# The adaLN projection moved from TensorE to GpSimd, and another order of rows in attention's output projection

## The chip, the cores and the metric

The kernel runs on one core of one Trainium2 chip. The metric is the device time of one execution in microseconds (us). A core has five engines that run side by side and wait for each other through semaphores: TensorE (PE; its weight loads are PEld), VectorE (DVE), ScalarE (ACT), GpSimd (POOL) and SyncE (SP), whose queue issues the weight loads from HBM here.

## The reference

Batch 1, 256 tokens, width 1024. A first block of two layers (pooling with attention and a gated FFN with a short convolution; RG-LRU and the same FFN) is followed by a second block whose two norms and two residuals are modulated (adaLN). The part of the reference that this change touches is `mod`; all it reads are the conditioning vector and its own weights, so it may be computed at any time before the second block:

```
x = first_block(x, ...)
c_act = silu(c)                                   # 1024 numbers
mod = c_act @ ada_w[l] + ada_b[l]                 # 1024 x 6144, in fp32
sh1, sc1, gt1, sh2, sc2, gt2 = split(mod, 6)
h = rms_norm_2(x, norm_mix_g[l]) * (1 + sc1) + sh1
...                                               # four mixers, merged
x = x + gt1 * (merged @ w_o[l])
h = rms_norm_2(x, norm_ffn_g[l]) * (1 + sc2) + sh2
x = x + gt2 * (square(relu(h @ ffn_w1[l])) @ ffn_w2[l])
```

Attention's output is `concat(pool_out, attn_out) @ pa_w_out`: 1024 rows, in 8 tiles of 128, by 1024 columns. Each FFN of the first block takes 1024 to 2 x 2816 columns (22 pairs of column tiles m and m + 22), convolves, gates, and goes back through 22 x 8 tiles.

## The kernel before

**Products.** All activations stand with features on the 128 partitions and the 256 tokens in the free dimension. Each large product is made of three fp32r matmuls (high x high, high x low, low x high). So every weight chunk of 128 x 1024 goes through three steps: SP loads it into a slot of `ring` (NR = 9 slots, in the order that `weight_order()` writes out), ACT rounds it to `whi` (NS = 7 buffers, 1 instruction), DVE subtracts to get `wlo` in place of the ring's slot (1 instruction with two operands in SBUF), and PE uses the two in 24 matmuls of 256 columns. One FFN column m of the input side is two chunks, m and m + 22: 48 matmuls.

**Order.** Each engine's program is written out by hand in the same nesting of stages: `pool_attn`, `conv_ffn(0)`, `rglru`, `conv_ffn(1)`, `mixers`, `relu_ffn`. ACT and DVE convert ahead through `feed(c)`, which goes up to AHEAD = 5 (DVE) or 6 (ACT) entries of the weight order past entry c; entries of the adaLN matrix count there, though nothing is converted for them. SP issues entry n when entry n - 9 has been used (`used`), strictly in order, so one late user holds all later loads. DVE's instructions of one FFN column are: subtract (`wlo`) for a later chunk, two taps of the convolution on `zu` (one operand in PSUM, one in SBUF), `wlo`, two taps on `zg`, then `hidl` and the product `zg<-zg,zu` (each with two operands in SBUF).

**adaLN.** The matrix `ada_w` is 48 chunks of 128 x 1024. A call of `mod_step` on PE takes two of them: four fp32 matmuls, each of 32 equal columns `sc32` (silu(c), spread) against 512 columns of the chunk, straight from the ring, accumulated in PSUM over 8 calls. Eight calls make a third of `mod`; ACT copies it to `mrow` and `mod_turn` turns it with four transposes. The 24 calls stand as `("A",)` in the table ATTN (7) and after the first column tile of attention's output projection (1), in `rglru` by ADA_RG (8), and in `conv_ffn(1)` by ADA_IN (8).

**End of attention.** The projection `pa_w_out` reads the tiles `pah`/`pal` 0 to 7. Tiles 4 to 7 come from the head pairs (steps O), 0 to 3 from the pooling groups (steps G, in the order 3, 2, 1, 0), and `linear` reads them in the order 0 to 7 for the first two column tiles together.

**GpSimd** adds the squares for the norms (`add_squares`, 6 small adds a norm), makes the masks and the pooling sums early in attention, and multiplies ten tiles in `rglru`.

## Time and profile before

| | |
|---|---|
| median of 3 runs | 1161.66 us (1161.20 to 1168.12) |
| the profiled execution, its own time | 1161.85 us |
| its span in the profile | 1160.0 us |
| PE busy, weight loads | 1091.7 us (94%), 1036.3 us (89%) |
| DVE, ACT, POOL busy | 835.9 us (72%), 641.7 us (55%), 66.7 us (6%) |
| mean granted TensorE clock | 0.976 |
| HBM read | 197.99 MB, 172 GB/s over the span |

The span is 1.85 us shorter than the execution's own time, and that in turn is 0.19 us over the median. A share of busy time is a mean over stages; the stages here run one after another: attention to 101 us, its output projection to about 134, the first FFN to 331, RG-LRU to 455, the second FFN to 655, then the second block.

### The profile page before, as it was taken

What the parts mean: (1) busy time and instruction counts of PE and PEld (TensorE: products, weight loads), DVE (VectorE), ACT (ScalarE), POOL (GpSimd) and SP (SyncE); (2) the same over time, 40 slices, a digit from 0 to 9 for tenths busy, and PEclk for the clock granted to TensorE, in tenths of its full rate; (3) what the DMA queues carried; (4) which work ended last, traced back from release to release, by engine and by line L of the source; (5) the groups of instructions that cost most, each with busy time, mean ns of one, the idle gap of its engine ahead of it and who ended that gap; (6) DMA issues with size and microseconds to landing.
All of it is one profiled execution on the core that took longest, in us unless ns stands there. A gap on an engine that the chain in (4) does not pass through costs nothing.

```text
span 1160.0 us, 21002 instructions
## 1 busy us (share of the span) xinstructions
PE 1091.7 (94%) x8588; PEld 1036.3 (89%) x8588; DVE 835.9 (72%) x1444; ACT 641.7 (55%) x1098; POOL 66.7 (6%) x79
## 2 busy tenths in 40 slices
PE   6996999999999979999999989899999979999996
PEld 6874999999987779999999978799989979999996
...
GB/s 344 120 203 235 128 213 185 184 171 180 193 215 186 276 133 135 247 237 228 237 220 185 195 111 107 83 92 91 128 109 155 70 207 179 182 183 183 184 160 37
DMA packets 59857, 200.41 MB, mean 173 GB/s; under 512 B 6769, under 2 KB 11505, under 8 KB 59633
## 3 DMA queue, kind: packets, MB, share of 16 engines
...
HBM read 197.99 MB, written 1.05 MB: 172 GB/s over the span
## 4 chain that ended last, share of the span: by engine, by line
PE 81%; DVE 10%; ACT 6%; DMA 1%; issue 1%; ACTq 0%; SPq 0%; POOL 0%; DVEq 0%
PE ps L470 80%; DVE wlo L1552 2%; ACT whi L1037 1%; ACT L1037 1%; DVE xr L1558 1%; DMA ring<-pa_w_out 1%; DMA ring<-pa_w_in 1%; ACT xr L1037 1%; DVE cosT L1552 1%; ACT rr L1037 0%; DVE rst L1581 0%; DVE raw L1552 0%; DVE bks L1552 0%; DVE hl L1552 0%; ACT sc L1037 0%
## 5 line engine op out<-in xcount | busy, mean ns | idle before, releaser
L470 PE MATMUL ps<-hh,whi 128*128 128x256 f32 (+1 forms) x1656 | 481.1, 291 | 18.1 <-DVE wlo L1552 15.6
L470 PE MATMUL ps<-hh,wlo 128*128 128x256 f32 (+1 forms) x1656 | 471.3, 285 | 0.0
L470 PE MATMUL ps<-hl,whi 128*128 128x256 f32 (+1 forms) x1656 | 469.4, 283 | 0.0
L1552 DVE TENSOR_TENSOR wlo<-ring,whi 128x1024 fp32r<-128x1024 f32 (+1 forms) x313 | 376.1, 1216 | 73.8 <-ACT whi L1037 73.2
L1037 ACT ACTIVATE whi<-ring 128x1024 fp32r<-128x1024 f32 (+1 forms) x313 | 321.6, 1039 | 68.7 <-PE ps L470 52.6
L470 PEld LDWEIGHTS ps<-hh,whi 128*128 128x128 f32 x1656 | 316.6, 191 | 39.0 <-issue 31.2
L470 PEld LDWEIGHTS ps<-hl,whi 128*128 128x128 f32 x1656 | 317.1, 192 | 1.3 <-issue 1.0
L470 PEld LDWEIGHTS ps<-hh,wlo 128*128 128x128 f32 x1656 | 316.7, 191 | 0.0
L470 PE MATMUL ps<-hidh,whi 128*128 128x256 f32 x608 | 172.2, 283 | 0.0
L470 PE MATMUL ps<-hidh,wlo 128*128 128x256 f32 x608 | 172.1, 283 | 0.0
L470 PE MATMUL ps<-hidl,whi 128*128 128x256 f32 x608 | 172.1, 283 | 0.0
L470 PEld LDWEIGHTS ps<-hidh,whi 128*128 128x128 f32 x608 | 116.7, 192 | 0.8 <-issue 0.8
L470 PEld LDWEIGHTS ps<-hidl,whi 128*128 128x128 f32 x608 | 116.7, 192 | 0.0
L470 PEld LDWEIGHTS ps<-hidh,wlo 128*128 128x128 f32 x608 | 116.7, 192 | 0.0
L2329 POOL TENSOR_TENSOR sqa<-sqa,sqt 128x256 f32<-128x256 f32 x36 | 34.5, 960 | 950.3 <-ACT sqt L1037 950.3
L1037 ACT ACTIVATE sqt<-x 128x256 f32<-128x256 f32 x49 | 20.1, 414 | 74.0 <-DVE x L1552 36.3
L1558 DVE SCALAR_TENSOR_TENSOR zg<-ps,vec,zg 128x255 f32<-128x255 f32 x84 | 40.4, 481 | 23.7 <-ACT zg L1037 21.1
L1037 ACT ACTIVATE zg<-ps,vec 128x256 f32<-128x256 f32 x42 | 23.6, 562 | 44.7 <-PE ps L470 44.6
L1037 ACT ACT_TABLE_LOAD x35 | 44.9, 1283 | 6.1 <-issue 3.9
L1558 DVE SCALAR_TENSOR_TENSOR zu<-ps,vec,zu 128x255 f32<-128x255 f32 x80 | 38.5, 481 | 12.1 <-ACT zu L1037 9.5
L1037 ACT ACTIVATE zu<-ps,vec 128x256 f32<-128x256 f32 x40 | 22.5, 564 | 29.7 <-PE ps L470 21.0
L470 PE MATMUL ps<-yin,ring 128*128 128x256 f32 x160 | 38.6, 378 | 0.0
...
## 6 DMA issues: line engine op xcount, KB each, us to landing
...
```

The lines of the kernel that those rows point to most:

```text
L470: return e.matmul(o, l, r, start=start, stop=stop)
L1037: return e.activation(o, i, func, bias=bias, scale=scale, accum_out=acc)
L1552: return e.tensor_tensor(o, a, b, op)
L1558: return e.scalar_tensor_tensor(out=o, in0=a, scalar=s, in1=b, op0=op0, op1=op1)
L2329: e.tensor_tensor(sqa[:, :], sqa[:, :], sqt[:, m % 2, :], ADD).then_inc(*sum_g.up((n, m)))
```

## The change

The 48 chunks of `ada_w` are used by GpSimd. For each, `mod_piece` multiplies the 128 x 1024 chunk by its column of silu(c) (one scalar for each partition) in place in the ring, and adds it to the running sum `acc` (the first of eight writes `acc` directly and has no addition). PE only adds over the partitions: `mod_sum`, two fp32 matmuls of 32 columns of ones against 512 columns of `acc`, six times in all, and the same three `mod_turn`. All pieces stand in the two FFNs: one chunk after each of 20 columns of the input side, and one after each of the first four columns of the output side. Attention, its projection and RG-LRU have none. SP's ring waits for GpSimd where an `ada_w` entry is replaced. `pa_w_out` reads its tiles in the order 4, 5, 6, 3, 2, 7, 1, 0.

```diff
-ADA_IN = ((), (2, 5, 8, 11, 14, 17, 19, 21))
-ADA_RG = ((5, 7, 9), (1, 3, 5, 7, 8))
+ADA_IN = (range(2, 22), range(1, 21))
+ADA_OUT = range(4)
+ADA_SUM = ({12: 0, 20: 1}, {11: 3, 19: 4})
+ADA_LAST = ({6: 2}, {5: 5})
+ADA_TURN = ({21: 0}, {12: 1})
...
-    13, ("B", 1), ("S", 3), ("P", 2), ("T", 1), ("A",), 14, ("S", 4), ("P", 3), ("T", 2), 15, ("S", 5), ("P", 4), ("T", 3), ("A",),
-    3, ("V",), ("S", 6), ("P", 5), ("T", 4), 2, ("O", 0), ("S", 7), ("P", 6), ("T", 5), ("A",), 1, ("O", 1), ("P", 7), ("T", 6),
-    ("A",), 0, ("T", 7), ("O", 2), ("G", 3), ("A",), ("G", 2), ("A",), ("O", 3), ("G", 1), ("A",), ("G", 0),
+    13, ("B", 1), ("S", 3), ("P", 2), ("T", 1), 14, ("S", 4), ("P", 3), ("T", 2), 15, ("S", 5), ("P", 4), ("T", 3),
+    3, ("V",), ("S", 6), ("P", 5), ("T", 4), 2, ("O", 0), ("S", 7), ("P", 6), ("T", 5), 1, ("O", 1), ("P", 7), ("T", 6),
+    0, ("T", 7), ("O", 2), ("G", 3), ("G", 2), ("O", 3), ("G", 1), ("G", 0),
...
-    ada = iter(range(24))
-
-    def columns():
-        n = next(ada)
-        o.extend(("ada_w", n, z, 0) for z in range(2))
+    ada = iter(("ada_w", 8 * r + k, z, 0) for r in range(3) for z in range(2) for k in range(8))
...
             whole("pa_w_in", 8, (at,))
-        elif at[0] == "A":
-            columns()
-        if m == 1:
-            columns()
...
             if m in ADA_IN[l]:
-                columns()
+                o.append(next(ada))
         for m in range(8):
             whole(f"ffn_w_out{l}", 22, (m,))
+            if m in ADA_OUT:
+                o.append(next(ada))
...
+        acc = [alloc(st, "acc", [128, 2, 1024])] * 2
...
-            def linear(w, ms, of, nk, need):
+            def linear(w, ms, of, nk, need, rows=range(8)):
-                    for q in range(n):
+                    for i, q in enumerate(rows[0:n]):
...
-                            t = mm(o, wlo[c % NR][:, q, :], rh, False, k + q == nk - 1)
-                            if q == n - 1:
+                            t = mm(o, wlo[c % NR][:, q, :], rh, False, k + i == nk - 1)
+                            if i == n - 1:
                                 t.then_inc(*through.up(c))
...
-            def mod_step():
-                n = ada["n"]
-                ada["n"] += 1
-                r, k = n // 8, n % 8
-                if k == 0:
-                    take(("ada", r))
-                p = ps[where["ada", r]]
-                for z in range(2):
-                    c = number["ada_w", n, z]
-                    landed[c % NR].wait_ge(e, c)
-                    ada_dve.wait_ge(e, "sc32")
-                    for y in range(2):
-                        g = 2 * z + y
-                        t = mm(p[32 * g:32 * g + 32, :], sc32[:, k, :], ring[c % NR][:, 4 * y:4 * y + 4, :], k == 0, k == 7)
-                    t.then_inc(*through.up(c))
-                if k == 7:
-                    give(("ada", r), ada_act, r)
-                    ada["late"] = r
-
-            def mod_turn():
-                r, ada["late"] = ada["late"], None
-                if r is not None:
-                    p = take(("mod", r))
-                    ada_act.wait_ge(e, r)
-                    for q in range(4):
-                        t = e.transpose(p[:, q * 128:q * 128 + 128], mrow[:, q * 128:q * 128 + 128], ident)
-                    t.then_inc(*ada_pe.up(r))
-                    give(("mod", r), ada_dve, ("mod", r))
+            def mod_sum(h):
+
+                r, z = h // 2, h % 2
+                p = take(("ada", h))
+                ada_pool.wait_ge(e, number["ada_w", 8 * r + 7, z])
+                for y in range(2):
+                    g = 2 * z + y
+                    t = mm(p[32 * g:32 * g + 32, :], ones[:, 0:32], acc[h // 3][:, z, y * 512:y * 512 + 512])
+                t.then_inc(*ada_pe.up(("sum", h)))
+                give(("ada", h), ada_act, h)
+
+            def mod_turn(r):
+                p = take(("mod", r))
+                ada_act.wait_ge(e, 2 * r + 1)
+                for q in range(4):
+                    t = e.transpose(p[:, q * 128:q * 128 + 128], mrow[:, q * 128:q * 128 + 128], ident)
+                t.then_inc(*ada_pe.up(("turn", r)))
+                give(("mod", r), ada_dve, ("mod", r))
...
-                residual(1, "pa_w_out", 8, pair(pah, pal), lambda k: at_dve.wait_ge(e, ("pal", k)), also)
+                residual(1, "pa_w_out", 8, pair(pah, pal), lambda k: at_dve.wait_ge(e, ("pal", k)), None, (4, 5, 6, 3, 2, 7, 1, 0))
...
-                    if m in ADA_IN[l]:
-                        mod_step()
+                    if m in ADA_SUM[l]:
+                        mod_sum(ADA_SUM[l][m])
+                    if m in ADA_TURN[l]:
+                        mod_turn(ADA_TURN[l][m])
...
                 def also(m):
-                    mod_turn()
+                    if m in ADA_LAST[l]:
+                        mod_sum(ADA_LAST[l][m])
+                    if l == 1 and m == 6:
+                        mod_turn(2)
...
-                    if m in ADA_RG[0]:
-                        mod_step()
...
-                    mod_turn()
-                    if m in ADA_RG[1]:
-                        mod_step()
...
 
             if order[c][0] == "rg_w_out" and order[c][2] == 9:
                 rg_pe.wait_ge(e, ("out", 7))
+            elif order[c][0] == "ada_w":
+                ada_pool.wait_ge(e, c)
             else:
                 through.wait_ge(e, c)
...
+            def mod_copy(h):
+                r, z = h // 2, h % 2
+                rows = slice(64 * z, 64 * z + 64)
+                ada_pe.wait_ge(e, ("sum", h))
+                if r:
+                    ada_pe.wait_ge(e, ("turn", r - 1))
+                act(mrow[rows, :], ps[where["ada", h]][rows, :], ACT.Copy).then_inc(*ada_act.up(h))
...
+            def scale_of(n):
+                ada_dve.wait_ge(e)
+                stt(gsc[:, n, :], mod[:, 24 * n + 8:24 * n + 16], 1.0, P(("norm_mix2", "norm_ffn2")[n], 0, 8), ADD, MUL).then_inc(*ada_dve.up(("gsc", n)))
...
+                        scale_of(0)
+                    if l == 1 and m == 6:
+                        mod_turn(2)
+                        scale_of(1)
...
+            def add_square(n, m):
+                square.wait_ge(e, (n, m))
+                sum_g.wait_ge(e)
+                e.tensor_tensor(sqa[:, :], sqa[:, :], sqt[:, m % 2, :], ADD).then_inc(*sum_g.up((n, m)))
...
-                    e.tensor_tensor(sqa[:, :], sqa[:, :], sqt[:, m % 2, :], ADD).then_inc(*sum_g.up((n, m)))
+                    add_square(n, m)
+
+            pieces = iter((h, k) for h in range(6) for k in range(8))
+
+            def mod_piece():
+
+                h, k = next(pieces)
+                c = number["ada_w", 8 * (h // 2) + k, h % 2]
+                a, w = acc[h // 3][:, h % 2, :], ring[c % NR][:, :, :].rearrange("p a b -> p (a b)")
+                ada_dve.wait_ge(e, "silu")
+                landed[c % NR].wait_ge(e, c)
+                if k == 0:
+                    if h > 1:
+                        ada_pe.wait_ge(e, ("sum", h - 2))
+                    e.tensor_scalar(a, w, cpar[15][:, k:k + 1], None, MUL).then_inc(*ada_pool.up(c))
+                else:
+                    e.tensor_scalar(w, w, cpar[15][:, k:k + 1], None, MUL).then_inc(*ada_pool.up(("product", c)))
+                    ada_pool.wait_ge(e)
+                    e.tensor_tensor(a, w, a, ADD).then_inc(*ada_pool.up(c))
+
+            def squares_and_pieces(n):
+                for m in range(8):
+                    if m in ADA_OUT:
+                        mod_piece()
+                    if 0 < m < 7:
+                        add_square(n, m)
...
-            add_squares(2)
+            for m in ADA_IN[0]:
+                mod_piece()
+            squares_and_pieces(2)
             for m in range(10):
...
             add_squares(3)
-            add_squares(4)
+            for m in ADA_IN[1]:
+                mod_piece()
+            squares_and_pieces(4)
             add_squares(5)
```

The weight order of SP at the end of attention, before: entries of `ada_w` stand among the last chunks of `pa_w_in` and those of `pa_w_out` (the number behind `ring` tells the slot).

```order
L2378 DMA ring_19<-pa_w_in 128x1024
L2378 DMA ring_20<-ada_w 128x1024
L2378 DMA ring_21<-ada_w 128x1024
L2378 DMA ring_22<-ada_w 128x1024
L2378 DMA ring_14<-ada_w 128x1024
L2378 DMA ring_15<-ada_w 128x1024
L2378 DMA ring_16<-ada_w 128x1024
L2378 DMA ring_17<-pa_w_out 128x1024
L2378 DMA ring_18<-pa_w_out 128x1024
L2378 DMA ring_19<-ada_w 128x1024
L2378 DMA ring_20<-ada_w 128x1024
L2378 DMA ring_21<-pa_w_out 128x1024
```

The same place in the changed kernel.

```order
L2362 DMA ring_20<-pa_w_in 128x1024
L2362 DMA ring_21<-pa_w_out 128x1024
L2362 DMA ring_22<-pa_w_out 128x1024
L2362 DMA ring_14<-pa_w_out 128x1024
L2362 DMA ring_15<-pa_w_out 128x1024
L2362 DMA ring_16<-pa_w_out 128x1024
```

The `pa_w_out` entries now follow the last `pa_w_in` entry directly, and each takes a slot that a `pa_w_in` entry nine places earlier leaves; the first `ada_w` entry comes behind all eight of them and six entries of the FFN.

PE at the end of attention, before: the pooling group G2, the head pair O3 (four PT rows), G1, G0, with adaLN steps (`sc`) between, then the projection.

```order
L470 MATMUL ps<-vf,pw 128x256
L470 MATMUL ps<-ring_22,sc_43 32x512 x2
L470 MATMUL ps<-ring_14,sc_43 32x512 x2
L470 MATMUL ps<-PT,vt 64x256
L470 MATMUL ps<-PT,vt 64x128
L470 MATMUL ps<-PT,vt 64x256
L470 MATMUL ps<-PT,vt 64x128
L470 MATMUL ps<-vf,pw 128x256
L470 MATMUL ps<-ring_15,sc_43 32x512 x2
L470 MATMUL ps<-ring_16,sc_43 32x512 x2
L470 MATMUL ps<-vf,pw 128x256
L470 MATMUL ps<-pah,whi_9 128x256
```

The same place in the changed kernel, from G3 on.

```order
L468 MATMUL ps<-vf,pw 128x256 x2
L468 MATMUL ps<-PT,vt 64x256
L468 MATMUL ps<-PT,vt 64x128
L468 MATMUL ps<-PT,vt 64x256
L468 MATMUL ps<-PT,vt 64x128
L468 MATMUL ps<-vf,pw 128x256 x2
L468 MATMUL ps<-pah,whi_9 128x256
L468 MATMUL ps<-pal,whi_9 128x256
```

The adaLN matmuls are gone; the rest stands in the same order, and the projection's first tile is another one (4 in place of 0, which the names don't show).

GpSimd around the first FFN, before: the end of the pooling sums, the 12 additions of squares of two norms in a row, then RG-LRU.

```order
L2344 TENSOR_TENSOR vf<-tb,u 128x256
L2338 TENSOR_TENSOR ta<-u 128x256
L2341 TENSOR_TENSOR ta<-ta,cst_56 128x256
L2344 TENSOR_TENSOR vf<-ta,u 128x256
L2329 TENSOR_TENSOR sqa<-sqa,sqt 128x256 x12
L2358 TENSOR_TENSOR ii<-ii,xr 128x256 x10
```

The changed kernel behind the first norm's squares, the first five pieces (two instructions for each but the first).

```order
L2280 TENSOR_TENSOR sqa<-sqa,sqt 128x256 x6
L2298 TENSOR_SCALAR acc<-ring_17,s5p 128x1024
L2300 TENSOR_SCALAR ring_20<-ring_20,s5p 128x1024
L2302 TENSOR_TENSOR acc<-ring_20,acc 128x1024
L2300 TENSOR_SCALAR ring_14<-ring_14,s5p 128x1024
L2302 TENSOR_TENSOR acc<-ring_14,acc 128x1024
L2300 TENSOR_SCALAR ring_17<-ring_17,s5p 128x1024
L2302 TENSOR_TENSOR acc<-ring_17,acc 128x1024
L2300 TENSOR_SCALAR ring_20<-ring_20,s5p 128x1024
L2302 TENSOR_TENSOR acc<-ring_20,acc 128x1024
```

24 such pieces stand between the two norms' squares, and 24 more in the second FFN.

## Rows read from the trace of the kernel before

**Rows 1.** The page, part 2: busy tenths in 40 slices of 29 us.

```profile
PE   6996999999999979999999989899999979999996
```

**Rows 2.** Timeline of PE at three adaLN steps of the second FFN: start us, us.

```profile
545.17 0.64 PE L470 MATMUL ps<-ring,sc 128*32 128x512 f32 x4
...
563.57 0.64 PE L470 MATMUL ps<-ring,sc 128*32 128x512 f32 x4
...
576.23 0.64 PE L470 MATMUL ps<-ring,sc 128*32 128x512 f32 x4
```

**Rows 3.** Chain of waits, end of attention: start us, us, what.

```profile
93.18 5.86 DMA ring<-pa_w_out
...
108.27 3.75 DMA ring<-pa_w_out
```

**Rows 4.** Windows, end of attention: busy time of each engine, granted clock, DMA.

```profile
core 0: us, PE busy (x) PEld busy (x) DVE busy (x) ACT busy (x) POOL busy (x), PEclk, DMA share, GB/s
95.80:101.10 5.30, 0.42 (x2) 0.04 (x2) 2.55 (x6) 3.10 (x4) 0.00 (x0) 1.00 0.96 367
101.10:109.00 7.90, 7.90 (x56) 7.45 (x56) 2.67 (x4) 1.65 (x3) 0.00 (x0) 0.78 0.07 26
109.00:113.60 4.60, 0.59 (x8) 0.00 (x0) 3.95 (x11) 2.96 (x7) 0.00 (x0) 0.77 0.94 328
113.60:118.30 4.70, 4.67 (x22) 4.67 (x23) 1.73 (x3) 2.03 (x4) 0.73 (x1) 0.50 0.31 126
```

**Rows 5.** Windows, second half of RG-LRU (columns as above).

```profile
383.00:420.00 37.00, 27.80 (x207) 23.15 (x205) 20.89 (x34) 36.01 (x70) 0.73 (x1) 0.89 0.72 241
```

**Rows 6.** Timeline of ACT near the end of RG-LRU.

```profile
412.98 1.99 ACT L1037 ACTIVATE whi<-ring 128x1024 fp32r<-128x1024 f32 x2
414.87 0.58 ACT L1037 ACTIVATE mrow<-ps 128x512 f32<-128x512 f32 x1
```

**Rows 7.** Timeline of DVE in one column of the first FFN, right after its start.

```profile
159.68 0.99 DVE L1558 SCALAR_TENSOR_TENSOR zu<-ps,vec,zu 128x255 f32<-128x255 f32 x2
160.59 1.22 DVE L1552 TENSOR_TENSOR wlo<-ring,whi 128x1024 fp32r<-128x1024 f32 x1
161.72 0.99 DVE L1558 SCALAR_TENSOR_TENSOR zg<-ps,vec,zg 128x255 f32<-128x255 f32 x2
162.63 0.42 DVE L1552 TENSOR_TENSOR hidl<-zg,hidh 128x256 fp32r<-128x256 f32 x1
...
164.43 0.99 DVE L1558 SCALAR_TENSOR_TENSOR zu<-ps,vec,zu 128x255 f32<-128x255 f32 x2
```

**Rows 8.** Waits of DVE, first FFN, 139.4 to 268.3 us: total, times, longest.

```profile
DVE zg L1558 <- ACT zg L1037: 10.0, 14, 0.9
```

**Rows 9.** Waits of DVE, second FFN, 455 to 597.5 us.

```profile
DVE zg L1558 <- ACT zg L1037: 11.1, 15, 1.3
DVE zu L1558 <- ACT zu L1037: 9.3, 7, 2.6
```

**Rows 10.** Timeline of PE and DVE where the first FFN's output side begins.

```profile
260.73 0.28 PE L470 MATMUL ps<-hidh,whi 128*128 128x256 f32 x1
...
264.99 0.43 DVE L1552 TENSOR_TENSOR hidl<-zg,hidh 128x256 fp32r<-128x256 f32 x1 [0.48 <-ACT hidh L1037]
```

**Rows 11.** Timeline of POOL, then of DVE: additions of squares beside `wlo`.

```profile
948.53 0.74 POOL L2329 TENSOR_TENSOR sqa<-sqa,sqt 128x256 f32<-128x256 f32 x1 [300.64 <-ACT sqt L1037]
951.28 1.59 POOL L2329 TENSOR_TENSOR sqa<-sqa,sqt 128x256 f32<-128x256 f32 x1 [2.01 <-ACT sqt L1037]
...
948.58 1.77 DVE L1552 TENSOR_TENSOR wlo<-ring,whi 128x1024 fp32r<-128x1024 f32 x1
...
951.06 1.21 DVE L1552 TENSOR_TENSOR wlo<-ring,whi 128x1024 fp32r<-128x1024 f32 x1
```

**Rows 12.** Timeline of POOL, then of DVE: multiplications for the masks beside `wlo`.

```profile
25.11 1.17 POOL L2351 TENSOR_SCALAR cosT<-cst 128x384 f32<-128x384 f32 x1
...
27.49 1.36 POOL L2351 TENSOR_SCALAR cosT<-cst 128x384 f32<-128x384 f32 x1
...
27.74 1.52 DVE L1552 TENSOR_TENSOR wlo<-ring,whi 128x1024 fp32r<-128x1024 f32 x1
```

100 lines of the change are left out of this document (24 added, 76 removed).

## The prediction

> **What bounds the kernel now.** I read the page first: PE is busy in nine tenths or more of most slices, and well short of that only in slices 3 and 14 (87 and 406 us) and at the ends [rows 1]. So most stages hang on PE's queue, and an instruction less there is worth its time; at those two something else is late. Then I read the adaLN steps on PE, the chain of waits and the windows at the end of attention, the window of RG-LRU's second half, and last DVE in the FFNs, because GpSimd is to work beside it there.
>
> A step's price on PE: steps with three columns between them start 18.40 us apart, with two columns 12.66 us apart [rows 2]; a column is the difference, 5.74, and a step 12.66 - 2 x 5.74 = 1.18 us. The kernel has 24 of them, 28 us.
>
> **The end of attention and its projection (gain).** Eight steps stand here: 8 x 1.18 = 9.4 us. Two further losses come from the ring: the chain goes through loads of `pa_w_out` at 93.18 and 108.27 us [rows 3], since `ada_w` entries hold slots until late steps and `pa_w_out` is issued behind them. PE stands still for 5.30 - 0.42 = 4.9 us, and again for 4.60 - 0.59 = 4.0 us [rows 4]. After each the granted clock falls: 0.78 over 7.9 us of work is 1.7 us lost, 0.50 over 4.7 us is 2.3 us [rows 4] (the clock's two levels are 1.2 and 2.4 GHz, and it fell both times behind a standstill). `mod_turn` leaves, four transposes at half clock: 0.6 us at full. In the new order every `pa_w_out` entry takes a slot of a long used `pa_w_in` entry, so it is there and converted before PE asks. What is late next is tile 0 (pool, ACT, DVE), but it is read last now, five tiles of 0.7 us behind the first, and I let 1 us stand. Sum 9.4 + 4.9 + 4.0 + 1.7 + 2.3 + 0.6 - 1 = **22 us**. The order of rows by itself is worth only that cover: if tile 0 were read first, about 2 us of waiting would remain. Bounds: 17 (no clock comes back and 1 us more stands) to 23.
>
> **RG-LRU (gain).** Of its eight steps one falls where DVE's taps are late, three on PE's path: 3.5 us. From 383 us on ACT is the bound, busy 36.0 of 37.0 us [rows 5], so the last four steps, which lie beside it, are worth nothing by themselves. But `feed` counts entries of the order, `ada_w` among them; with none there about three more conversions come before 383 us, when ACT has room, 0.95 us each (1.99 for two [rows 6]), and the copy to `mrow`, 0.58 [rows 6], leaves ACT. 3.5 + 2.9 + 0.5 = 6.9; I take **6.5**, between 3.5 and 7.
>
> **The FFNs (loss).** PE loses eight steps in the second, 9.4 us, and gets six sums. A sum is half a step's matmuls, 0.6 us; those in the output sides and the turn count for 1.5 us together. What decides is GpSimd beside DVE.
>
> What the trace shows of the two: alone, POOL adds 256 columns in place in 0.74 us; begun 0.22 us behind the start of a `wlo` of 1.21 us it took 1.59 and ended 0.6 us behind it: it waited for the whole of it. The other way round, a `wlo` begun 0.05 us after POOL's addition took 1.77 in place of 1.21 [rows 11]: it waited 0.56 us, nearly all of the addition. So two instructions with both operands in SBUF exclude each other, in either order. DVE's taps have one operand in PSUM and go on. An addition of 1024 columns should hold DVE for 4 x 0.55 = 2.2 us. A multiplication on POOL (one tile in) is milder: 384 columns took 1.17 us alone, 1.36 beside `wlo`, and `wlo` took 1.52 [rows 12], 0.31 us more. So it holds DVE for 0.31 us at its start, and works on for 0.8 us beside it. For 1024 columns that is 0.31 x 1024 / 384 = 0.83 us of hold; its length is 1.9 us if the 0.8 is fixed and 3.1 if all grows with the columns.
>
> The Trainium skill (SBUF — State Buffer, Who interferes with whom) says that a VectorE instruction with two SBUF inputs contends with a GpSimd one that reads SBUF, and that whoever starts first holds the shared ports for the whole instruction. The additions agree, 1.77 against 1.21; the multiplications don't, since `wlo` lost 0.31 us and not 1.1. The same skill's GPSIMD Engine Reference (Engine selection) calls one-input work there roughly line-rate; at 1.17 us for 384 columns this trace shows a third of that, so the page speaks for the short length, and by it the time would be the lower edge given below, 1147.5.
>
> Now a column of DVE when it never waits: 4.75 us from one pair of taps to the same of the next (159.68 to 164.43), made of `wlo` 1.13, two taps 0.91, `wlo` 1.13, two taps 0.91, and `hidl` and the product, 0.34 each [rows 7]. I laid POOL beside it. The addition gets in at the end of a `wlo`, 2.2 us: the taps run beside it, the next `wlo` waits 2.2 - 0.91 = 1.29. The multiplication gets in behind that `wlo`, and its hold of 0.83 is covered by the next taps. If it is short, the addition is ready again before the following `wlo` ends, and the pattern repeats: 1.29 us a piece. If long, the addition begins 0.45 us into the taps and the wait is 1.74. I take the middle, **1.5 us** for a piece, as nothing tells the lengths apart; both ends go into the range.
>
> Per FFN 17 full pieces on the input side give 25.5 us. Three have no addition, 0.3 each, 0.9. At the start DVE has only two-operand work (norm and its halves), where two pieces hold it fully: 2 x (3.03 - 1.5) = 3.1. Together 29.5 us of delay. Against it stands DVE's slack. In the first FFN it waits 10.0 us for taps [rows 8] and 2.3 in three smaller rows of that answer; its last `hidl` ends at 265.42, and PE, which begins the output side at 260.73 [rows 10], needs that row 63 matmuls of 0.12 later, at 268.2: 2.8 more. Slack 15.1, loss 29.5 - 15.1 = 14.4 us. In the second it waits 11.1 + 9.3 us [rows 9], 1.0 in smaller rows and 2.5 at the end, 23.9, which holds the 9.4 us of the steps: loss 5.6 us. The four pieces on each output side find DVE with 1.8 us of room in each of PE's 7.9 us, and I cost them at nothing.
>
> Ring and POOL itself: a piece takes 1.9 to 3.1, 2.4, and waits of about 1, so 5.3 to 6.5 us, against columns that then take 6.1 to 6.5. The ring lets a piece be landed two columns before it must be gone. Costed at nothing; if that fails it is a rival.
>
> **Sum.** 1161.85 (the profiled execution) - 22 - 6.5 + 14.4 + 5.6 + 1.5 = 1154.8. Against the median this is 0.2 less: **1154.6 us**. With 1.29 us a piece both FFNs lose 17 x 0.21 = 3.6 us less, 1147.5; with 1.74 they lose 4.1 more each, 1163.
>
> **Rivals.**
> *DVE is hardly held* (chance 0.25). POOL may yield within a long instruction, or fall into step so that its holds lie under taps; a delay of 0.5 us a piece makes 12.4 us an FFN, less than the slack. Then the first FFN only gets its sums (1.5 us), the second gains 8, and the whole is 1161.85 - 28.5 - 8 + 3 = 1128. For it: taps are 1.82 of 4.75 us. Against it: both orders of the additions were exclusive [rows 11]. Between this and the forecast all values occur; its middle is 1137.
> *The multiplication holds DVE for its whole length* (0.18). Then the column is `wlo` 1.13, addition 2.2, `wlo` 1.13, multiplication 1.9 to 3.1, small ones 0.68: 7.0 to 8.2 us, a delay of 2.3 to 3.5 a piece, 45 to 68 us an FFN with the start. Losses 30 + 21, or 53 + 44; the time 1185 to 1231. It is slower than before from 1.7 us a piece (0.2 more in 34 pieces is the 7 us that the forecast leaves), by over 1% from 2.05. The 384-column rows speak against it, but 1024 columns may not fit whatever let those be read ahead. The Trainium skill's section on who interferes with whom, cited above, states this rule for all such pairs.
> *POOL sets the pace through the ring* (0.10). If a piece with its waits takes 7.5 us (3.1 + 2.4 + two waits of 1), 20 of them take 150 us where PE's columns took 115; less 13 us of ring and start that is 22 us an FFN, from which the second had 9.4 to give: 1161.85 - 28.5 + 22 + 12.6 + 1.5 = 1169 and up to 1180. SP would then wait for POOL in front of `ffn_w_in`.
> *PE's clock falls in the FFNs* (0.04): PE would stand still for 0.4 to 0.8 us a column. In the windows it fell only behind 4 to 5 us [rows 4]. It would be over 1180.
> *The forecast's own case*, 1.29 to 1.74 us a piece, 1147 to 1163, has 0.43.
>
> **How the numbers follow.** A difference within 1% (11.6 us) is about what measurement of this kernel tells from none. Faster by over 1% (under 1150.0): 0.25 and the lower edge of my case, 0.10. Slower by over 1% (over 1173.3): 0.18, 0.04, and half of the ring's, 0.05, 0.27. Within: 0.38. For 8 in 10 the range leaves out the last tenth of each side: 1133 to 1197.
>
> **What would show it.** The projection beginning near 88 us, no standstill over 2 us before 120, no half clock there; RG-LRU shorter by 6 to 7 us. POOL busy some 120 us in each FFN's input side, an addition of 1024 columns near 2.4 us alone, the multiplication telling 1.9 from 3.1. DVE without waits for taps through both input sides, `wlo` at a mean of 1.5 to 1.7 us there, columns of 6.1 to 6.5 us, PE waiting for `wlo`. Wrong would be: columns of 5.74 (DVE not held), over 7 (held in full), or PE and SP waiting for POOL.

## Result and the profile after

The changed kernel takes 1170.9 us (median of 6 runs, 1167.16 to 1173.34) against 1161.27 us (1160.28 to 1168.12): a ratio of 1.0072, 95% interval 1.0053 to 1.009. It is slower by 0.7%, where 0.6% faster was forecast. Its profiled execution took 1171.93 us, its span is 1170.1.

The kernel has natural marks on PE: the first matmul that reads a stage's inputs (`pah` for attention's projection, `sqa` for a norm, `hidh` for an FFN's output side, and so on). Their starts in the two traces give the length of each stage, and a length taken from the sum of the forecast stands beside it:

| stage | before | after | difference | forecast |
|---|---|---|---|---|
| attention, to the projection | 101.1 | 88.3 | -12.8 | |
| projection | 34.5 | 25.6 | -8.9 | both -22 |
| 1st FFN, input side | 125.1 | 141.0 | +15.9 | +14.4 |
| 1st FFN, output side | 65.6 | 76.5 | +10.9 | 0 |
| RG-LRU, two stages | 93.8 | 84.7 | -9.1 | -6.5 |
| its projection | 34.9 | 35.0 | +0.1 | |
| 2nd FFN, input side | 134.8 | 141.5 | +6.7 | +5.6 |
| 2nd FFN, output side | 66.1 | 73.1 | +7.0 | 0 |
| all behind | 493.3 | 493.6 | +0.3 | 0 |
| sums and turn in output sides | | | | +1.5 |

Attention with its projection and the two input sides are near the forecast; RG-LRU returned 9.1 us, over the upper bound of 7. Two rows are far off: the output sides lose 17.9 us where 1.5 was put. Between the forecast's 1154.8 and the profiled execution's 1171.93 lie 17.1 us, and the output sides account for 16.4 of them.

Every length is of one execution, the profiled one. How much it can vary is seen from e11 below, whose program is the same in both FFNs: its output sides took 74.6 and 69.9 us, so there the loss is 12.8 us, not 17.9.

The windows of the changed kernel (columns as in [rows 4]), first the projection, a stretch of RG-LRU, then each FFN's input side and the first 9.8 or 10 and the next 6.8 us of each output side:

```profile
core 0: us, PE busy (x) PEld busy (x) DVE busy (x) ACT busy (x) POOL busy (x), PEclk, DMA share, GB/s
88.30:113.90 25.60, 25.57 (x212) 25.33 (x211) 21.07 (x54) 16.79 (x31) 5.32 (x7) 1.00 0.48 155
383.00:410.00 27.00, 21.42 (x176) 21.11 (x175) 13.21 (x22) 26.06 (x51) 0.74 (x1) 0.96 0.48 156
113.90:254.90 141.00, 132.76 (x1054) 128.03 (x1055) 138.96 (x185) 79.39 (x137) 119.01 (x39) 0.99 0.69 232
254.90:264.70 9.80, 8.05 (x63) 7.64 (x63) 8.81 (x16) 3.85 (x9) 5.78 (x2) 1.00 0.64 201
264.70:271.50 6.80, 6.28 (x27) 5.99 (x28) 6.63 (x12) 5.01 (x8) 0.00 (x0) 0.50 0.48 154
...
451.10:592.60 141.50, 132.35 (x1054) 128.59 (x1055) 139.09 (x185) 81.80 (x139) 113.66 (x39) 0.98 0.69 234
592.60:602.60 10.00, 8.06 (x65) 7.64 (x63) 9.26 (x15) 3.31 (x8) 6.72 (x2) 1.00 0.51 149
602.60:609.40 6.80, 6.21 (x30) 5.99 (x29) 6.16 (x12) 3.74 (x7) 0.00 (x0) 0.50 0.47 154
```

Against [rows 4] the projection has no standstill (25.57 of 25.60 us busy, clock 1.00). In the input sides DVE is busy for 138.96 of 141.00 us: it has become the bound, and PE waits. In the output sides something else is seen, 27 matmuls in 6.8 us at half clock, behind 9.8 us in which PE stood still for 1.8. The standstills come again in other executions of this FFN program; the half clock doesn't always (below).

How GpSimd holds DVE in the input side is shown by a column of the changed kernel, the timeline of POOL and then of DVE:

```profile
203.05 3.82 POOL L2300 TENSOR_SCALAR ring<-ring,s5p 128x1024 f32<-128x1024 f32 x1
206.95 2.41 POOL L2302 TENSOR_TENSOR acc<-ring,acc 128x1024 f32<-128x1024 f32 x1
```

```profile
201.41 2.74 DVE L1522 TENSOR_TENSOR wlo<-ring,whi 128x1024 fp32r<-128x1024 f32 x1
204.07 0.99 DVE L1528 SCALAR_TENSOR_TENSOR zg<-ps,vec,zg 128x255 f32<-128x255 f32 x2
204.98 0.43 DVE L1522 TENSOR_TENSOR hidl<-zg,hidh 128x256 fp32r<-128x256 f32 x1
205.33 0.41 DVE L1522 TENSOR_TENSOR zg<-zg,zu 128x256 f32<-128x256 f32 x1
205.67 1.21 DVE L1522 TENSOR_TENSOR wlo<-ring,whi 128x1024 fp32r<-128x1024 f32 x1
206.80 0.98 DVE L1528 SCALAR_TENSOR_TENSOR zu<-ps,vec,zu 128x255 f32<-128x255 f32 x2
207.71 2.74 DVE L1522 TENSOR_TENSOR wlo<-ring,whi 128x1024 fp32r<-128x1024 f32 x1
```

From one held `wlo` to the next, 201.41 to 207.71, is 6.30 us where [rows 7] has 4.75: one `wlo` of two takes 2.74 in place of 1.21, 1.53 us for a piece. It ends at 210.45, the addition at 209.36, 1.1 us (a `wlo`'s own length) sooner: the `wlo` waited for the addition, and the taps at 206.80 had run beside it. The `wlo` at 205.67 began inside a multiplication and took its usual 1.21; here it is the multiplication that takes 3.82 us where 2.85 is its length alone (e7), and it ends when that `wlo` does, at 206.87. This is the pattern laid out by hand in the forecast. That the size agrees to 0.03 us is in part luck: 1.5 was the middle between a short multiplication (1.29) and a long one (1.74). It was long, and the addition began 0.15 us into the taps and not 0.45.

### The profile page after: what moved, and what is told of

Same layout as the page of the kernel before. It is cut to its first block, busy times and chain, and to the rows that moved or that the text cites. A ratio compares the mean times of both kernels' runs of the same rounds, so it can differ in the third digit from the quotient of the medians.

```text
span 1170.1 us, 20767 instructions
## 1 busy us (share of the span) xinstructions
PE 1082.7 (93%) x8420; PEld 1039.9 (89%) x8420; DVE 914.8 (78%) x1443; ACT 638.7 (55%) x1101; POOL 336.8 (29%) x169
## 3 DMA queue, kind: packets, MB, share of 16 engines
HBM read 197.99 MB, written 1.05 MB: 170 GB/s over the span
## 4 chain that ended last, share of the span: by engine, by line
PE 47%; DVE 38%; ACT 8%; issue 5%; DMA 1%; ACTq 0%; SPq 0%; DVEq 0%
PE ps L468 47%; DVE wlo L1522 16%; DVE zg L1528 3%; DVE zu L1528 3%; DVE hidl L1522 2%; ACT whi L1019 2%; ACT L1019 2%; DVE zg L1522 1%; DVE hl L1528 1%; DVE w L1522 1%; DVE raw L1528 1%; DVE xr L1528 1%; DVE hl L1522 1%; DVE x L1522 1%; DVE rst L1551 1%
## 5 line engine op out<-in xcount | busy, mean ns | idle before, releaser
L1522 DVE TENSOR_TENSOR wlo<-ring,whi 128x1024 fp32r<-128x1024 f32 (+1 forms) x313 | 436.8, 1408 | 50.1 <-ACT whi L1019 49.4
L468 PE MATMUL ps<-hidh,whi 128*128 128x256 f32 x608 | 175.7, 289 | 6.9 <-DVE hidl L1522 4.7
L2300 POOL TENSOR_SCALAR ring<-ring,s5p 128x1024 f32<-128x1024 f32 x42 | 141.8, 3377 | 50.8 <-DMA ring<-ada_w 50.5
L468 PEld LDWEIGHTS ps<-hidh,whi 128*128 128x128 f32 x608 | 119.2, 196 | 10.3 <-DVE hidl L1522 5.7
L468 PEld LDWEIGHTS ps<-hidl,whi 128*128 128x128 f32 x608 | 119.2, 196 | 0.0
L468 PEld LDWEIGHTS ps<-hidh,wlo 128*128 128x128 f32 x608 | 119.1, 196 | 0.0
L2302 POOL TENSOR_TENSOR acc<-ring,acc 128x1024 f32<-128x1024 f32 x42 | 105.2, 2504 | 3.5
L1528 DVE SCALAR_TENSOR_TENSOR x<-ps,mod,x 128x256 f32<-128x256 f32 x16 | 7.6, 482 | 41.2 <-PE ps L468 41.2
```

The lines of the kernel that those rows point to most:

```text
L468: return e.matmul(o, l, r, start=start, stop=stop)
L1522: return e.tensor_tensor(o, a, b, op)
L1528: return e.scalar_tensor_tensor(out=o, in0=a, scalar=s, in1=b, op0=op0, op1=op1)
L2300: e.tensor_scalar(w, w, cpar[15][:, k:k + 1], None, MUL).then_inc(*ada_pool.up(("product", c)))
L2302: e.tensor_tensor(a, w, a, ADD).then_inc(*ada_pool.up(c))
```

## What the runs told apart

Lengths of the four FFN stages in all kernels, from the same marks and one profiled execution each (us), with each kernel's median; the kernel before had 1161.17 to 1162.49 beside them. e1, e5 to e10 and e13 leave out part of GpSimd's arithmetic, so they tell causes and are no versions to use.

| kernel | time | ratio, 95% interval | 1st in | 1st out | 2nd in | 2nd out |
|---|---|---|---|---|---|---|
| before | 1161.27 | | 125.1 | 65.6 | 134.8 | 66.1 |
| after | 1170.9 | 1.0072, 1.0053 to 1.009 | 141.0 | 76.5 | 141.5 | 73.1 |
| e1 no arithmetic | 1135.35 | 0.9773, 0.9759 to 0.9788 | 129.4 | 66.8 | 132.7 | 67.1 |
| e2 halves | 1169.57 | 1.0071, 1.0052 to 1.0091 | 143.1 | 73.2 | 144.9 | 68.9 |
| e3 on DVE | 1149.23 | 0.9894, 0.9875 to 0.9913 | 134.5 | 70.5 | 134.9 | 68.5 |
| e4 PE in the FFNs | 1151.46 | 0.9914, 0.9896 to 0.9932 | 144.6 | 65.7 | 134.9 | 66.1 |
| e5 output side free | 1158.07 | 0.9955, 0.9938 to 0.9972 | 142.1 | 66.8 | 142.3 | 67.1 |
| e6 input side free | 1140.91 | 0.9812, 0.9798 to 0.9827 | 129.4 | 71.9 | 132.7 | 67.1 |
| e7 multiplications only | 1140.58 | 0.9807, 0.9792 to 0.9821 | 129.4 | 68.0 | 133.4 | 67.1 |
| e8 additions only | 1156.6 | 0.9954, 0.9938 to 0.9971 | 140.5 | 69.8 | 140.7 | 68.4 |
| e9 first piece of the output | 1160.71 | 0.9994, 0.9978 to 1.001 | 143.5 | 68.1 | 141.9 | 68.9 |
| e10 last two | 1162.29 | 1.0003, 0.9989 to 1.0016 | 142.1 | 70.7 | 141.3 | 67.1 |
| e11 rows in order | 1171.51 | 1.0102, 1.0064 to 1.0141 | 141.0 | 74.6 | 140.8 | 69.9 |
| e12 DVE and PE | 1151.49 | 0.991, 0.9893 to 0.9926 | 132.2 | 71.2 | 136.3 | 71.5 |
| e13 first two | 1166.68 | 1.0039, 1.0022 to 1.0056 | 140.0 | 71.7 | 142.3 | 70.0 |
| e14 DVE late | 1149.44 | 0.9899, 0.9882 to 0.9915 | 135.7 | 69.0 | 138.1 | 67.1 |

### All of the arithmetic: e1

```
-                    e.tensor_scalar(w, w, cpar[15][:, k:k + 1], None, MUL).then_inc(*ada_pool.up(("product", c)))
-                    ada_pool.wait_ge(e)
-                    e.tensor_tensor(a, w, a, ADD).then_inc(*ada_pool.up(c))
+                    e.tensor_scalar(w[:, 0:8], w[:, 0:8], cpar[15][:, k:k + 1], None, MUL).then_inc(*ada_pool.up(c))
```

> The changed kernel with GpSimd's arithmetic left out: the first piece of each eight still multiplies 8 columns only, the others too, and nothing is added up, so the modulation is made of other numbers. All 48 chunks are loaded, hold their ring slots and are released by GpSimd at the same places, and PE and ACT do their sums and copies. Theory A (GpSimd's instructions hold DVE at the SBUF ports): both input sides go back to PE's 5.74 us a column, the output sides to 7.9 us a tile, and the time is 1161.3 - 21.7 (attention) - 9.0 (RG-LRU) - 9.4 (steps gone from the second FFN) + 3 (sums) = about 1124 us. Theory B (the loads moved into the FFNs, and the ring entries that take places in the look-ahead, are what slows them): the FFNs stay as slow as in the changed kernel, 1165 to 1171 us.

Measured 1135.35 us: 35.6 us hang on GpSimd's arithmetic, by subtraction 11.6 and 8.8 in the input sides and 9.7 and 6.0 in the output sides. It is also 11 us over the 1124 that was expected, and that is a second finding. The second FFN's input side should have shed all of its eight steps, 9.4 us, and shed 2.1; the first took 4.3 us more than before. One part is in the waits of PE from 430 to 450 us of e1:

```profile
PE ps L468 <- DVE wlo L1522: 3.1, 1, 3.1
```

The kernel before has 0.2 us there. Behind that wait the granted clock is 0.50 for 3.4 us from 446.8 (1.7 us of work lost), where the kernel before has 1.00. Another is a wait of 1.1 us at 114.65 us for the last square of the norm. The third part is the sums, which I had priced at 0.6 us. One in the changed kernel:

```profile
246.75 1.05 PE L468 MATMUL ps<-acc,cst 128*32 128x512 f32 x4
```

It takes about 1.07 us out of PE's row of matmuls, and there are two in each input side. In the first side 2.1 for the sums and the wait of 1.1 are 3.2 of the 4.3; in the second 2.1 + 3.1 + 1.7 = 6.9 of the missing 7.3. The rest is open. The entries of the order between the chunks (20 in 20 columns, before 16 in eight of them) shorten how far `feed` converts ahead; that this makes the 3.1 us was not tried apart.

### Multiplication or addition: e7, e8, e2

e7 leaves out the line of the addition, e8 that of the multiplication (but for the first of each sum), e2 writes the addition as two of 512 columns:

```
-                    e.tensor_tensor(a, w, a, ADD).then_inc(*ada_pool.up(c))
+                    e.tensor_tensor(a[:, 0:512], w[:, 0:512], a[:, 0:512], ADD)
+                    e.tensor_tensor(a[:, 512:1024], w[:, 512:1024], a[:, 512:1024], ADD).then_inc(*ada_pool.up(c))
```

> GpSimd's additions are left out, all 48 multiplications stay at 1024 columns. Theory A (a multiplication holds VectorE for a fraction only, 0.3 to 0.8 us, and much of it falls under the taps): VectorE held for 0 to 10 us an FFN, less than its slack; the time 1135 to 1142. Theory B (it holds VectorE for its whole 2.85 us): 17 x 1.9 us or more an FFN beside the taps' cover, the time 1150 or more, and wlo at 2.5 us or more in every column.

> GpSimd's multiplications with the scalar are left out except the first of each sum, so it adds the raw entries; the 42 additions stay at 1024 columns. Theory A (an addition costs its 2.2 us of hold less the 0.91 of the taps under which it runs on): 1.29 us a piece instead of the 1.5 measured with multiplications, VectorE held 26 to 29 us an FFN instead of 35; the time 1160 to 1166. Theory B (the multiplication before it is what made the addition meet wlo, alone it falls under the taps): held under 15 us, the time 1140 to 1150.

> The changed kernel with each addition of 1024 columns on GpSimd written as two of 512. The same reads in all, but each instruction holds the ports for 1.1 us, not 2.2. Theory A (an instruction holds DVE for its whole length, and 0.91 us of it is covered by a pair of taps): two pairs of taps cover in place of one, so some 0.2 + 0.2 us remain of the additions, and the multiplication's 0.83 may now fall on the small two-operand instructions; 1.0 to 1.3 us a piece in place of 1.53, 5 us less in each FFN, 1158 to 1164 us. Theory B (ring and loads): no change, 1170 us, or 2 more for the extra instructions.

e7 came out at 1140.58 as theory A has it. Groups of instructions of e7 and then of e8, DVE's two forms that can be held and POOL's two (out<-in, count, busy us, mean ns):

```profile
L2300 POOL TENSOR_SCALAR ring<-ring,s5p 128x1024 f32<-128x1024 f32 x42 | 129.8, 3090 | 126.4 <-DMA ring<-ada_w 126.4
...
L1522 DVE TENSOR_TENSOR wlo<-ring,whi 128x1024 fp32r<-128x1024 f32 x281 | 347.9, 1244 | 43.5 <-ACT whi L1019 42.8
L1522 DVE TENSOR_TENSOR hidl<-zg,hidh 128x256 fp32r<-128x256 f32 x44 | 20.2, 459 | 1.8 <-ACT hidh L1019 1.8
```

```profile
L2301 POOL TENSOR_TENSOR acc<-ring,acc 128x1024 f32<-128x1024 f32 x42 | 106.6, 2538 | 162.9 <-DMA ring<-ada_w 162.8
...
L1522 DVE TENSOR_TENSOR wlo<-ring,whi 128x1024 fp32r<-128x1024 f32 x281 | 374.3, 1339 | 45.1 <-ACT whi L1019 44.4
L1522 DVE TENSOR_TENSOR hidl<-zg,hidh 128x256 fp32r<-128x256 f32 x44 | 40.0, 910 | 1.8 <-ACT hidh L1019 1.8
```

In e1 these means are 1235 and 416. 42 multiplications of some 3 us add 9 ns to each of 281 `wlo` and 43 ns to each of 44 `hidl`, 4.4 us together. The additions add 104 and 494 ns, 51 us. One place of e7 shows how mild a multiplication is, timelines of POOL and of DVE:

```profile
207.41 2.85 POOL L2300 TENSOR_SCALAR ring<-ring,s5p 128x1024 f32<-128x1024 f32 x1 [3.09 <-DMA ring<-ada_w]
```

```profile
209.67 1.22 DVE L1522 TENSOR_TENSOR wlo<-ring,whi 128x1024 fp32r<-128x1024 f32 x1
```

The `wlo` begins 2.26 us into a multiplication of 2.85 us and takes its usual 1.22: it is not held. Only some that begin in a multiplication's first microsecond are. One of them, again POOL and DVE of e7:

```profile
136.91 3.15 POOL L2300 TENSOR_SCALAR ring<-ring,s5p 128x1024 f32<-128x1024 f32 x1 [1.93 <-DMA ring<-ada_w]
```

```profile
137.34 2.06 DVE L1522 TENSOR_TENSOR wlo<-ring,whi 128x1024 fp32r<-128x1024 f32 x1
```

It is held for 2.06 - 1.22 = 0.84 us and not for the 2.7 that the multiplication goes on; the forecast had 0.83 for this hold. This is where the Trainium skill's section on who interferes with whom (SBUF — State Buffer) would have it wait; for additions its rule agrees with the trace (2.74 against 1.21), for a multiplication with one tile and a scalar per row it doesn't: the longest that one held a `wlo` in e7's trace is 0.9 us (2.10 at 218.60), and not the whole instruction.

e8 came out between its ranges, at 1156.6: DVE is held some 31 us (the excess of its instructions over their undisturbed length, summed) in each input side, nearly the 33.6 and 33.3 of the changed kernel, so theory A's size is right and theory B's (under 15) isn't. The additions stand elsewhere in the output sides, which are 6.7 and 4.7 us shorter than the changed kernel's. e2 missed: halves were expected to slip between DVE's instructions and gain 7 to 13 us. They hold DVE just as long, now in three places of a column in place of one, and the time is 1169.57.

So a piece on GpSimd costs DVE 33.6 / 20 = 1.7 us of its time, on the mean of 20 of which three have no addition. How that compares with doing it there is e3.

### The same work elsewhere: e3, e4

e3 issues the piece on DVE, behind the same column, in one instruction; GpSimd has none:

```
+                    stt(a, w, cpar[15][:, k:k + 1], a, MUL, ADD).then_inc(*ada_pool.up(c))
```

> The changed kernel with the pieces on DVE itself: one instruction for each chunk, chunk times scalar plus acc, at the end of the same columns; GpSimd has no piece. Theory A: it costs DVE 1.13 us of its own in place of 1.53 us of being held, so the input sides are some 19 to 21 us of DVE work heavier instead of 35: the first FFN's loses 4 to 6 us, the second's gains 3, and the time is 1135 to 1142 us. Theory B: as slow as the changed kernel, since DVE's work grows and the ring is the same, 1168 to 1175 us.

Measured 1149.23: faster than before (0.9894), but 7 us above the range; the first input side lost 9.4 us where 4 to 6 were expected, and the second gained nothing where 3 were. The price of a piece, groups of instructions of e3:

```profile
L1528 DVE SCALAR_TENSOR_TENSOR acc<-ring,s5p,acc 128x1024 f32<-128x1024 f32 x42 | 53.6, 1277 | 0.0
```

1.28 us. DVE loses less by doing the whole piece than by being held while GpSimd does it (1.7 us). The output sides lose 4.9 and 2.4 us against before, 1.07 of it in each by the sum.

e4 keeps the kernel before's products on PE, puts 16 steps into the first FFN's input side and leaves eight in the second; attention and RG-LRU have none, and the rows of the projection are read in the new order.

```
+ADA_IN = ((2, 3, 4, 5, 7, 8, 9, 10, 12, 13, 14, 15, 17, 18, 19, 20), (2, 5, 8, 11, 14, 17, 19, 21))
+ADA_RG = ((), ())
```

> The kernel before with its own adaLN steps on PE, only moved: none in attention, its projection and RG-LRU, 16 in the first FFN's input side, 8 in the second's as before; the projection reads its tiles in the changed order. It tells what the change's other half, the new place, is worth without GpSimd. Attention and projection -21.7, RG-LRU -9.0, the first FFN + 16 x 1.18 = 18.9: 1149.5 us. If the ring entries or the loads slow the FFN (theory B), there are 32 of them on the first input side and it would be 1160 or more.

Measured 1151.46, 2 us over the number expected and far from theory B's 1160. Placement by itself is worth 11 us; the first FFN pays 19.5 us for 16 steps (1.22 each), the two stages where they stood return more.

### The output sides: e5, e6, e9, e10, e13

Each is the changed kernel with a condition ahead of the arithmetic under which a piece multiplies only 8 columns; for e5:

```
+                if k and k > 3 and h in (2, 5):
+                    w = w[:, 0:8]
+                    e.tensor_scalar(w, w, cpar[15][:, k:k + 1], None, MUL).then_inc(*ada_pool.up(c))
```

> The four pieces of each output side keep their ring entries and signals, but GpSimd multiplies only 8 columns in each and adds nothing; the 40 of the input sides are whole. Theory C (the 10.9 and 7.0 us that the output sides lost are carried over: VectorE comes late out of the input side, TensorE takes the first tiles in bites and its clock halves): output sides stay at 73 to 75 and 71 to 73 us, the time 1165 to 1170. Theory P (they are lost to the pieces that stand there, which hold hl and wlo): output sides fall to 67 and 67 us, the time 1155 to 1158.

> The reverse: of the 40 pieces of the input sides only the six first ones of a sum are whole, the others multiply 8 columns and add nothing; the four of each output side are whole. Theory C: nothing is carried over, the four pieces find room, output sides 67 to 70 us, the time 1136 to 1141. Theory P: output sides 75 and 72 us, the time 1149 to 1152. The two runs together with e1 (neither) and the changed kernel (both) make a square; if the sizes do not add up, the pieces and the backlog act on each other.

My theory was C, a backlog carried over; as the whole cause it fell. With the four pieces light the output sides are 66.8 and 67.1 us, as with no arithmetic at all, though the input side is as long as ever (142.1 and 142.3) and DVE comes out of it as late; the time, 1158.07, is at the edge of P's range. The pieces that stand there are needed for the loss. But e6 doesn't give what P expects: its time, 1140.91, lies in C's range, and with the input side light the pieces cost 5.1 us and nothing. The two act on each other: the pieces cost more when DVE comes late out of the input side. e9 and e10 take the four apart.

> Of the four pieces of each output side only the first is whole; the other three multiply 8 columns and add nothing. Theory F (in the changed kernel the addition of this first piece begins just ahead of the hidl of the last rows, holds it for 2.1 us, TensorE, which asks for those rows at once, goes on in bites and its clock halves): output sides 72 to 74 and 70 to 72 us against 66.8 and 67.1 with none whole, the time 1164 to 1168. Theory S (the loss is spread evenly over the four pieces): 69 and 69 us, the time 1160 to 1162.

> The first two pieces of each output side multiply 8 columns and add nothing, the last two are whole. Theory F: the last two find VectorE with room, output sides 67 to 69.5 us each, the time 1158 to 1161. Theory S: 71.5 and 70 us, the time 1163 to 1166.

e9, 1160.71 with 68.1 and 68.9 us, is what theory S has, and well under theory F; e10, 1162.29 with 70.7 and 67.1, is neither's. F failed because I had the wrong piece. GpSimd runs the first of the four some 7 us ahead of the output side, as soon as its entry has landed. The one on the last `hidl` is the second, and it was light in both. What is seen of it in the changed kernel, timeline of POOL and of DVE:

```profile
257.65 3.41 POOL L2300 TENSOR_SCALAR ring<-ring,s5p 128x1024 f32<-128x1024 f32 x1 [3.98 <-DMA ring<-ada_w]
261.14 2.37 POOL L2302 TENSOR_TENSOR acc<-ring,acc 128x1024 f32<-128x1024 f32 x1
```

```profile
261.32 2.48 DVE L1522 TENSOR_TENSOR hidl<-zg,hidh 128x256 fp32r<-128x256 f32 x1 [0.40 <-ACT hidh L1019]
263.72 0.41 DVE L1522 TENSOR_TENSOR zg<-zg,zu 128x256 f32<-128x256 f32 x1
264.61 0.42 DVE L1522 TENSOR_TENSOR hidl<-zg,hidh 128x256 fp32r<-128x256 f32 x1 [0.48 <-ACT hidh L1019]
```

The addition begins 0.18 us before the `hidl` of row 20 and keeps it to 263.8; row 21 is made behind it. PE has been asking for row 20 since 262.3 and gets it at 263.8, 1.5 us later; for row 21 it waits 0.6 us more. Now the windows of e5 over the same 9.8 and 6.8 us behind the start of its output side, to be read against 254.90:264.70 and 264.70:271.50 above:

```profile
256.00:265.80 9.80, 9.80 (x84) 9.80 (x83) 8.85 (x17) 5.76 (x11) 0.47 (x1) 1.00 0.71 210
265.80:272.60 6.80, 6.80 (x59) 6.80 (x59) 5.58 (x11) 3.42 (x5) 0.00 (x0) 1.00 0.79 279
```

84 + 59 = 143 matmuls against 63 + 27 = 90: 53 fewer, at 9.8 / 84 = 0.117 us each 6.2 us, 2.5 us in the first stretch, by standstills, and 3.7 in the second, where PE stands for 0.5 us and works the rest at half clock.

What belongs to the pieces and what to the clock, e11's trace tells. Its FFNs run the same program, and PE's standstills there are the same to 0.03 us (0.7, 1.5 and 0.6 us, the last two from 263.57 and 265.69, and one more of 0.5). The same two stretches behind the start of its first output side:

```profile
256.10:265.90 9.80, 8.05 (x63) 7.67 (x63) 8.81 (x16) 3.82 (x9) 5.80 (x2) 1.00 0.65 201
265.90:272.70 6.80, 5.88 (x46) 5.67 (x47) 6.63 (x12) 5.47 (x8) 0.00 (x0) 1.00 0.63 183
```

The clock stays at 1.00, with 46 matmuls where the changed kernel's execution had 27. So the pieces bring the standstills, and the half clock behind them came in one execution and not in the other. 6.8 us at half clock are 3.4 us of work. Without it there e11's output sides are 74.6 and 69.9 us, 7.8 and 2.8 over e5's: that much is the pieces' own. Of the other kernels with the moved pieces only e13 has half clock near the start of an output side, 3.4 us in the first; the rows of the rest can be compared without it.

> The first two pieces of each output side are whole, the last two multiply 8 columns and add nothing. In the traces of e9 and e10 the first of the four runs some 7 us ahead of the output side and the second is the one whose addition stands on the last rows' hidl. Theory F, with the right piece: output sides 71.5 to 73.5 and 72 to 74 us (with the first alone 68.1 and 68.9, with the last two alone 70.7 and 67.1), half clock behind the bites near 264 and 602 us, the time 1165 to 1169. Rival: the sizes only add up when all four are whole, because the delay of one tile reaches the next; then 69 and 69.5 us, the time 1160 to 1163.

e13 has it in the first FFN: 1166.68 us, output sides 71.7 and 70.0. The second is 2 us under its range, with no half clock near 602. Its windows over the same stretches of the first (the second one is at 0.75, since half of it ran at half clock):

```profile
253.60:263.40 9.80, 8.04 (x63) 7.66 (x63) 8.81 (x16) 3.81 (x9) 5.76 (x2) 1.00 0.64 203
263.40:270.20 6.80, 5.86 (x34) 5.66 (x35) 6.63 (x12) 5.46 (x8) 0.00 (x0) 0.75 0.48 154
```

The second piece is 71.7 - 68.1 = 3.6 us of the first FFN, 1.7 of it by the 3.4 us at half clock and 1.9 by itself; the first is 1.3, the last two 3.9 (in the changed kernel a `wlo` of 896 columns takes 3.29 us and an `hl` of the next norm 2.63 beside them, for 1.08 and 0.47). Without the clock's part that is 66.8 + 1.3 + 1.9 + 3.9 = 73.9 of e11's 74.6. In the second FFN the sum gives 67.1 + 1.8 + 1.1 + 0 = 70.0, and e11 has 69.9. The changed kernel's 73.1 is 3.1 us more, about the 3.4 that 6.8 us at half clock cost: that rest is mostly the clock in its profiled execution (and a first standstill of 1.3 us where e11 has 0.7), and no effect of the four together that every execution has. Each part is a difference of single executions, so a few tenths of it mean nothing.

### The rest: e11, e12, e14

e11 is the changed kernel without the order of rows:

```
-                residual(1, "pa_w_out", 8, pair(pah, pal), lambda k: at_dve.wait_ge(e, ("pal", k)), None, (4, 5, 6, 3, 2, 7, 1, 0))
+                residual(1, "pa_w_out", 8, pair(pah, pal), lambda k: at_dve.wait_ge(e, ("pal", k)))
```

> The changed kernel with the projection of attention reading its rows 0 to 7 in order. The forecast put about 2 us on that edit: 1172 to 1174, with a wait of about 2 us for tile 0 near 88 us. The rival is that the tile is ready anyway: 1171 and no wait.

PE's waits of e11 from 86 to 115 us:

```profile
PE ps L468 <- DVE pal L1528: 1.1, 1, 1.1
```

So the edit covers 1.1 us, not 2, and of the 1 us that the forecast let stand nothing is left (the changed kernel has no wait there). The times, 1165.17 to 1178.01, are too wide to tell. The profiled execution is the fastest of them.

e12 and e14 try to beat e3. In e12 DVE does six of a sum's eight pieces and PE multiplies two (four where the sum reaches the output side) with `sc32` into the bank in which the sum ends; in e14 PE takes only the four pieces of the last four columns of an input side.

```
+ADA_PE = [(4, 5, 6, 7) if h % 3 == 2 else (6, 7) for h in range(6)]    e12
+ADA_PE = [(0, 1, 2, 3) if h % 3 == 2 else () for h in range(6)]        e14
...
+                        t = mm(p[32 * g:32 * g + 32, :], sc32[:, k, :], ring[c % NR][:, 4 * y:4 * y + 4, :], k == ADA_PE[h][0], False)
```

> A version that should beat all so far. GpSimd does none of the pieces. In a sum's eight pieces VectorE multiplies and adds the first six in one instruction each (1.28 us of VectorE, less than the 1.6 to 1.7 us for which a piece on GpSimd holds it), and TensorE multiplies the last two itself (two matmuls of 0.6 us... per pair of halves, 0.6 us a piece), into the bank in which the sum then ends; of the sum that reaches into the output side it takes the last four, so that VectorE has no piece there. Expected against e3: first input side 134.5 to 132, output sides 70.5 and 68.5 to 69.2 and 69.5, second input side 135: 1145 to 1148. Rival: TensorE's pieces wait for late entries of the ring and give back what VectorE gains, 1150 or more.

> As e3, all pieces off GpSimd, but TensorE multiplies the four pieces that stand in the last four columns of each input side, and VectorE those of the output side, so that VectorE comes to the last rows without the backlog for which TensorE waited twice for 0.5 us with half clock behind it in e3. Against e3 (134.5, 70.5, 134.9, 68.5): input sides 134 to 137, output sides 67 to 69: 1146 to 1150. Rival: what TensorE's four pieces cost (2.4 to 4.4 us an FFN, by e12) takes all of it back, 1151 or more.

e12, 1151.49, is the rival's number but not for its reason: but for 0.8 us at the norm's sum (113.5) PE has no standstill up to the end of the first FFN. Its own pieces cost 71.2 - 66.8 = 4.4 us for the four in the output side, where 0.6 us each was put. The price came from the kernel before's steps. One of them, and then one piece of e12:

```profile
545.17 1.06 PE L470 MATMUL ps<-ring,sc 128*32 128x512 f32 x8
```

```profile
254.65 1.05 PE L470 MATMUL ps<-ring,sc 128*32 128x512 f32 x4
```

A step works on two chunks and a piece on one, and they take 1.06 and 1.05 us: halving the step saved next to nothing, just as a sum is half a step's matmuls and takes 1.05 us. Four such pieces are 4.2 of the 4.4 us. PE pieces that take two chunks at a time, as the kernel before does, were not tried in e12's places.

e14, 1149.44, removes the two waits of 0.5 us behind e3's first FFN input side (its expectation speaks of half clock behind them; in e3's trace the clock is 1.00 from 246.7 to 262 us), and its output sides are 1.5 and 1.4 us shorter than e3's; its input sides are 1.2 and 3.2 longer. Three kernels end within 0.2% of each other (0.9894, 0.9899, 0.991), and e3, the simplest, is the version to take.

## Why the forecast was wrong

**The step that failed** is "The four pieces on each output side find DVE with 1.8 us of room in each of PE's 7.9 us, and I cost them at nothing", with the ring's and the sums' 1.5 us the whole of what was put there. It cost 17.9 us in the profiled execution. Room on DVE was the wrong thing to ask for. Held instructions there are those for which PE waits at once: the last rows' `hidl`, a `wlo`, and `hl` of the norm. With e1's 66.8 and 67.1 the two sums take 2.2 us of the 17.9 (1.07 each, where a sum was put at 0.6), and the pieces with the clock behind them 15.7. Of these 10.6 are the pieces' own (7.8 + 2.8, by e11, whose execution had no half clock at the start of these stages), and the other 5.1 came with the half clock and, in the second FFN, a standstill 0.6 us longer. Without the pieces (e5) the time is 1158.07, 3.5 us above my number.

**The clock added to it**, in some executions. I had "In the windows it fell only behind 4 to 5 us", and gave short gaps in the FFNs 0.04. In the profiled execution it fell to 0.50 for 6.8 us at 264.7, behind gaps of 0.7, 1.5 and 0.6 us, and again at 602.6. Behind the same gaps of the first FFN it fell for 3.4 us in e13 and not at all in e11. So a fall behind short gaps happens, which the remark excluded, but isn't sure. The rival had its mechanism and its place wrong (it meant gaps in every column, where PE's gaps of 0.3 us left the clock at 1.00 from 140 to 254 us), so it isn't the case that came about.

**Attention and its projection**, -21.7 for 22: right, standstills and half clocks gone as read from [rows 3, 4]. The reserve of 1 us for tile 0 wasn't needed, and the order of rows covers 1.1 us.

**RG-LRU**, -9.1 for 6.5: right in sign, too small, over my upper bound of 7. In the window of ACT that I took for the bound it is busy 26.06 of 27.00 us from 383 to 410; the stage ends earlier than the conversions that I counted explain, and I have not taken this apart; the cause of the 2.6 us more stays open.

**The input sides**, +15.9 and +6.7 for 14.4 and 5.6: near, but by two errors against each other. DVE was held for 33.6 and 33.3 us, not 29.5, with 1.53 us a piece in the steady pattern as forecast; the difference is in the first columns and where an addition stands on `hidl` instead. And of the 15.9 us only 11.6 hang on GpSimd's arithmetic, the other 4.3 (and, in the second, 7.3 of the 9.4 that the steps should have returned) come with the sums and start waits that e1 shows and that I had put at nothing in the input sides. The slack that I subtracted was in turn larger than 15.1: 33.6 us of holding cost 11.6. In the second FFN most of PE's standstill lies at its start. PE's waits of the changed kernel from 451 to 593 us:

```profile
PE ps L468 <- DVE wlo L1522: 7.3, 8, 5.3
```

The 5.3 us are one wait at 466.4 us, and the clock is 0.50 for 6.8 us from 469.5; before, PE waits 0.2 us in the first 21 us of this stage, at clock 1.00. That GpSimd holds DVE in full at the start was in the forecast, at 3.1 us of DVE's time; that PE stands there in one piece, and what follows on the clock, was not.

**The rivals.** The multiplication that holds DVE in full is out (e7: 4.4 us on `wlo` and `hidl` for 42 of them). Its length is 2.85 us alone, 3.8 beside `wlo`, the long end; the addition is 2.4. Its hold of 0.83 us at the start is seen as 0.84. DVE hardly held is out (e8). The ring: SP waited for GpSimd for 1.0 us in all, so it is out as a pace. That GpSimd's help could be worth less than nothing to DVE itself, 1.7 us held against 1.28 us to do the work, I didn't compare, though both prices could have been estimated from `wlo`. In [rows 1] slice 32 (928 us) is a 7 as well, beside the two that I named; it lies in the second block, which the change doesn't touch (+0.3 us).
